# A hybrid attention, recurrence and mixture-of-experts layer on one core: fillers and ones-matmuls in the attention loop, another order at the hand-over, row gathers one turn later

## The reference

```
proj = x @ w_in                      # q, k, v of 8 attention heads; q, f, i, g of 8 recurrence heads
a = moba_attention(q, k, v, t5_bias) # causal block-sparse softmax attention, blocks of 256 keys
r = rms(hgrn2(q, f, i)) * norm_w * sigmoid(g)
x = layer_norm(alpha * x + concat(a, r) @ w_o)
g = top-1 of softmax over 4 groups;  e = top-2 of its 4 experts
y = sum over experts of weight * ((silu(x @ w_gate[e]) * (x @ w_up[e])) @ w_down[e])
x = layer_norm(alpha * x + y)
```

## Time and profile before

| | |
|---|---|
| median of 3 runs | 619.5 us (619.29 to 619.69) |
| the profiled execution, its own time | 619.69 us |
| its span, first to last instruction | 617.9 us |
| PE busy | 594.8 us (96%) |
| DVE busy | 479.2 us (78%) |
| ACT busy | 373.9 us (61%) |
| POOL busy | 127.1 us (21%) |
| mean granted TensorE clock | 0.987 |

### The profile page before, as it was taken

One profiled execution on the slowest core, in us unless ns is written; L12 is line 12 of the kernel. 1 busy time (PEld: TensorE's weight loads), 2 busy tenths in 40 slices (PEclk: granted clock), 3 DMA queues, 4 the chain that ended last, 5 costly groups with the idle time before them and its releaser, 6 DMA issues.

```text
span 617.9 us, 9761 instructions
## 1 busy us (share of the span) xinstructions
PE 594.8 (96%) x3691; PEld 479.2 (78%) x3691; DVE 479.2 (78%) x572; ACT 373.9 (61%) x401; POOL 127.1 (21%) x111
## 2 busy tenths in 40 slices
PE   8999999999999999999799999999999999999990
PEld 6878888888787678876688888888888888888870
DVE  3748598893577765556888989888888988888867
ACT  3659434432215983214378777877877787787735
POOL 0004222290000440000464722111110011111000
PEclk9999999999999999999899999999999999999996
DMA  8821133223206003975789999999999999999754
GB/s 326 294 97 66 62 126 124 77 73 77 70 2 204 3 2 132 416 282 205 247 321 420 418 372 368 390 389 390 408 406 390 389 389 387 392 409 404 249 171 136
DMA packets 42557, 155.77 MB, mean 252 GB/s; under 512 B 11939, under 2 KB 12147, under 8 KB 30236
## 3 DMA queue, kind: packets, MB, share of 16 engines
q1 hardware_dynamic: 37500, 138.40, 57.5%
q0 software_dynamic: 5024, 16.92, 10.6%
HBM read 139.96 MB, written 15.34 MB: 251 GB/s over the span
## 4 chain that ended last, share of the span: by engine, by line
PE 85%; DMA 6%; DVE 5%; issue 3%; ACT 1%; DVEq 0%; SPq 0%; POOLq 0%; ACTq 0%
PE psum L658 24%; PE psum L660 22%; PE psum L659 22%; DMA acc_dram<-misc,slots 3%; PE psum L771 2%; PE psum L1053 2%; PE psum L888 2%; PE psum L911 2%; PE psum L875 2%; DMA ring<-acc_dram 1%; PE psum L1070 1%; PE psum L667 1%; DVE w_lo L1775 1%; DMA cst<-in_c_main 1%; PE psum L813 1%
## 5 line engine op out<-in xcount | busy, mean ns | idle before, releaser
L1775 DVE TENSOR_TENSOR w_lo<-ring,w_hi 128x2048 fp32r<-128x2048 f32 x95 | 217.6, 2305 | 23.4 <-ACT w_hi L1345 21.1
L658 PE MATMUL psum<-w_hi,act_hi 128*128 128x512 f32 x544 | 219.6, 404 | 1.7 <-DVE act_lo L1934 1.0
L660 PE MATMUL psum<-w_hi,act_lo 128*128 128x512 f32 x544 | 213.0, 392 | 0.0
L659 PE MATMUL psum<-w_lo,act_hi 128*128 128x512 f32 x544 | 212.8, 391 | 0.0
L1345 ACT ACTIVATE w_hi<-ring 128x2048 fp32r<-128x2048 f32 x96 | 182.1, 1916 | 26.2 <-PE psum L660 25.1
L658 PEld LDWEIGHTS psum<-w_hi,act_hi 128*128 128x128 f32 x544 | 102.8, 189 | 28.3 <-DVE w_lo L1775 5.0
L660 PEld LDWEIGHTS psum<-w_hi,act_lo 128*128 128x128 f32 x544 | 102.4, 188 | 22.1
L659 PEld LDWEIGHTS psum<-w_lo,act_hi 128*128 128x128 f32 x544 | 102.7, 189 | 19.3
L612 POOL DMA_INDIRECT acc_dram<-misc,slots x15 | 23.9, 1596 | 192.7 <-ACT misc L1395 176.0
L1193 ACT ACTIVATE w_hi<-ring 128x2048 fp32r<-128x2048 f32 x17 | 32.6, 1917 | 49.1 <-PE psum L660 47.4
L1504 DVE TENSOR_TENSOR w_lo<-ring,w_hi 128x2048 fp32r<-128x2048 f32 x17 | 39.8, 2345 | 22.3 <-ACT w_hi L1193 22.1
(11 more groups left out here) (246 smaller groups left out, 686.5 us busy)
## 6 DMA issues: line engine op xcount, KB each, us to landing
ring<-in_w_gate SPq DMA_DIRECT2D x32, 1024.0 KB, 19.8
ring<-in_w_up SPq DMA_DIRECT2D x32, 1024.0 KB
ring<-in_w_down SPq DMA_DIRECT2D x32, 1024.0 KB, 20.5
ring<-in_w_in SPq DMA_DIRECT2D x13, 1024.0 KB, 5.4
ring<-in_w_o SPq DMA_DIRECT2D x4, 1024.0 KB, 6.7
acc_dram<-ring SPq DMA_DIRECT2D x5, 512.0 KB
ring<-in_x SPq DMA_DIRECT2D x2, 1024.0 KB, 6.5
ring<-strip_dram SPq DMA_DIRECT2D x8, 256.0 KB, 4.8
```

What stands on the lines that cost most here:

```text
L658: pe.matmul(dst, lh, rh, start=first, stop=False, skip_group_check=True)
L659: pe.matmul(dst, lh, rl, start=False, stop=False, skip_group_check=True)
L660: return pe.matmul(dst, ll, rh, start=False, stop=last, skip_group_check=True)
L1775: dve.tensor_tensor(w_lo[:, v0 % WBUF, :], ring[:, slot, :], w_hi[:, v0 % WBUF, :].bitcast(F32), ALU.subtract).then_inc(s_lo, 1)
```

## The change

It has three parts.

1. Attention loop. The scores of step 1 go to banks 4 and 5, with a wait for the logits of units 0 and 1, and `probs_t` loses its first two waits. 12 fillers stand ahead of the scores of step 1, and 10 each behind the scores of steps 1, 2 and 3. POOL writes diagonal 128x128 tiles (identity x reciprocal) into 8 buffers in place of the `wide` blocks, with a wait for the spread before, and `spread_scale` multiplies ones with them, in 8 matmuls in place of 4 transposes. `centred_router` moves from n = 8 to n = 4 on DVE.
2. Hand-over. SP's list of DMAs has another order and one wait more, for gather 1.
3. Expert loop. POOL issues gather(e + 2) in turn e in place of gather(e + 3).

```diff
@@ score banks, and the tiles
-        wide = misc[:, 3072:4096].rearrange("p (b i c) -> p b i c", b=2, i=T)
+        diag = misc[:, 3072:4096].rearrange("p (n c) -> p n c", c=P)
...
-            return (6 if step == 1 else 4 if step == 0 or step % 2 == 1 else 2) + n % 2
+            return (4 if step == 0 or step % 2 == 1 else 2) + n % 2
@@ SP
             expert_unit(step[5], 1, 0, 0)
-            sp.wait_ge(s_x1last, 1)
-            keep_tile(T - 1)
             sp.wait_ge(s_x1t, T + 1)
             sp.wait_ge(s_cent, T)
             expert_unit(step[3], 1, 0, 10)
+            sp.wait_ge(s_x1last, 1)
+            keep_tile(T - 1)
             sp.wait_ge(s_x1out, 16 * T)
-            sp.wait_ge(s_xg[0], 16)
-            expert_unit(step[4], 1, 0, 11)
+            for b in range(2):
+                sp.wait_ge(s_xg[b], 16)
             keep_sum(T - 1, T - 1)
             keep_sum(T - 1, T)
+            expert_unit(step[4], 1, 0, 11)
             sp.wait_ge(s_acc, 16 * (T + 1))
             expert_unit(step[0], 2, 1, 1)
@@ POOL
                 pool.wait_ge(s_prec, n // 2 + 1)
-                if n >= 4 * T:
-                    pool.wait_ge(s_scale, n // (2 * T) - 1)
-                pool.tensor_scalar(wide[:, n // (2 * T) % 2, i, 64 * (h % 2):64 * (h % 2) + 64], ones[:, 0:64], prec[:, col:col + 1], None, ALU.mult).then_inc(s_wide, 1)
+                if n >= DIAGS:
+                    pool.wait_ge(s_scale, 2 * (n // DIAGS))
+                pool.tensor_scalar(diag[:, n % DIAGS, :], ident, prec[:, col:col + 1], None, ALU.mult).then_inc(s_diag, 1)
...
             for e in range(NE - 1):
-                if EARLY < e + 3 < NE:
-                    gather(e + 3)
+                if EARLY < e + 2 < NE:
+                    gather(e + 2)
@@ PE
             def scores(n):
...
-                if n >= 6:
+                if n == 2:
+                    pe.wait_ge(s_logit, n)
+                elif n >= 6:
                     pe.wait_ge(s_logit, n - 2)
...
             def probs_t(n):
...
-                if n < 2:
-                    pe.wait_ge(s_logit, n + 3)
...
             def spread_scale(a):
...
                 for i in range(T):
-                    last = pe.transpose(psum[:, (a + 1) % 2, i * P:(i + 1) * P], wide[:, a % 2, i, :], ident)
-                last.then_inc(s_scale, 1)
+                    for par in range(2):
+                        last = pe.matmul(psum[64 * par:64 * par + 64, (a + 1) % 2, i * P:(i + 1) * P], ones[:, 0:64], diag[:, 2 * i + par, :],
+                                         start=True, stop=True, skip_group_check=True)
+                        if i == T - 1:
+                            last.then_inc(s_scale, 1)
...
             for n in range(0, NU + 4, 2):
+                if n == 2:
+                    keep_warm(12, 6)
                 if n < NU:
                     scores(n)
-                if n == 2:
+                if 2 <= n < 8:
                     pe.wait_ge(s_qklo, 2 * PAIRS)
-                    pe.wait_ge(s_router, 2)
-                    pe.matmul(psum[:, 1, 0:2 * KD * NL], ones, wg_b.rearrange("p r k n -> p (r k n)"), start=True, stop=True).then_inc(s_wsum, 1)
-                if n == 12:
+                    if n == 2:
+                        pe.wait_ge(s_router, 2)
+                        pe.matmul(psum[:, 1, 0:2 * KD * NL], ones, wg_b.rearrange("p r k n -> p (r k n)"), start=True, stop=True).then_inc(s_wsum, 1)
+                    keep_warm(10, 0)
+                if n == 10:
                     pe.wait_ge(s_router, 5)
@@ DVE
-                if n == 8:
+                if n == 4:
                     centred_router()
```

More of the change, by code:

```diff
@@ L48 @@
 EARLY = 4
+DIAGS = 8
 UNIT = 2048
@@ L320, in build @@
         s_tab, s_strip, s_stripsb, s_stripd, s_strips = sem("s_tab"), sem("s_strip"), sem("s_stripsb"), sem("s_stripd"), sem("s_strips")
-        s_score, s_logit, s_prob, s_wide, s_pt, s_ptsb, s_pv = sem("s_score"), sem("s_logit"), sem("s_prob"), sem("s_wide"), sem("s_pt"), sem("s_ptsb"), sem("s_pv")
+        s_score, s_logit, s_prob, s_diag, s_pt, s_ptsb, s_pv = sem("s_score"), sem("s_logit"), sem("s_prob"), sem("s_diag"), sem("s_pt"), sem("s_ptsb"), sem("s_pv")
         s_mixt, s_mixthi, s_mixtlo = sem("s_mixt"), sem("s_mixthi"), sem("s_mixtlo")
@@ L561, in _, with inverse_diagonal @@
                                pad_i[:, :, :]).then_inc(s_pads, 16)
-            def inverse_spread(n):
+            def inverse_diagonal(n):
                 h, i = unit(n)
@@ L567, in inverse_spread @@
                 pool.wait_ge(s_prec, n // 2 + 1)
-                if n >= 4 * T:
-                    pool.wait_ge(s_scale, n // (2 * T) - 1)
-                pool.tensor_scalar(wide[:, n // (2 * T) % 2, i, 64 * (h % 2):64 * (h % 2) + 64], ones[:, 0:64], prec[:, col:col + 1], None, ALU.mult).then_inc(s_wide, 1)
+                if n >= DIAGS:
+                    pool.wait_ge(s_scale, 2 * (n // DIAGS))
+                pool.tensor_scalar(diag[:, n % DIAGS, :], ident, prec[:, col:col + 1], None, ALU.mult).then_inc(s_diag, 1)
             for n in range(NU):
-                inverse_spread(n)
+                inverse_diagonal(n)
             def gather(e):
@@ L891, in spread_scale @@
             def spread_scale(a):
-                pe.wait_ge(s_wide, 2 * T * (a + 1))
+                pe.wait_ge(s_diag, 2 * T * (a + 1))
                 if a >= 1:
@@ L1710, in scale_kept @@
             def scale_kept(a):
-                dve.wait_ge(s_scale, a + 1)
+                dve.wait_ge(s_scale, 2 * (a + 1))
                 dve.tensor_copy(scale_row, bank((a + 1) % 2)).then_inc(s_mixa, 1)
```

## The result

The changed kernel takes 627.2 us at the median (625.5 to 628.8, 4 runs), the kernel before 619.4 in the same job: ratio 1.0122, with a 95% interval of 1.0095 to 1.0149. A later job of four runs gave 625.9 us and 1.0098 (1.0082 to 1.0113). With the profiled execution and one more, its ten executions took 625.5 to 628.8 us, 626.1 at the median. The forecast was 632.5, its range 625.0 to 635.5. So it is slower, by half to three fifths of the 13 us forecast. Two slow executions, one of the kernel before (843.5 us) and one of e2 (1186.5 us), enter no comparison.

The account below looks back on a forecast made before the run. PE, busy for 96% of the span, was taken to set the pace. Attention 6.0, gather 5's wait 5.5 and clock 1.5 made 13.0 us on 619.69, so 632.7, or 632.5 from the median; range 625.0 to 635.5.

Parts of the forecast that it names:

- gather(5) lands in time: Rival, expert loop: expert 5's rows land without making PE wait, leaving 619.5 + 6.0 = 625.5 us; 12%.
- First wait, 0.85: Attention, step 1: scores wait for logits of units 0 and 1, twelve fillers hidden under it; +0.85 us, bounds 0.4 and 1.3.
- Fillers, 3.3: Attention: 3 x 10 fillers between pieces of PE's chain, not hidden, 0.11 us each; +3.3 us, bounds 0 and 4.9.
- The rival of hidden fillers: Attention: unseen holes on PE hide the fillers, so 632.5 - 3.3 = 629.2 us; 6%.
- Spread, 1.9: Attention: eight matmuls at 1.02 us replace four transposes at 0.59, 0.44 in the last spread; +1.9 us, all on PE.
- attention's 6.0: Attention in all: 0.85 + 3.3 + 1.9 = +6.0 us on PE, shifting everything behind it.
- Clock in attention: Attention: granted clock already 1.00, so fillers and ones-matmuls have no lost clock to buy back.
- Hand-over, 0 (bound + 1): Hand-over: SP's new order delays the last x1 tile, covered by some 1 us; zero, without cover up to +1.
- Gather 5, 5.5, and its clock, 1.5: Expert loop: PE waits once for expert 5's rows, +5.5 us (4.3 to 5.9), then low clock, +1.5 (0 to 2).
- The margin in every turn: Rival, expert loop: the 2 us margin fails, gathers 6 to 15 cost 1 us each; 642.5 us, 5%.
- Clock, 1.5, elsewhere: Hand-over low clock, six matmuls costing 1.2 us, taken as model for +1.5 us behind expert 5's wait.

Follow-up runs that it names:

- e2: Kernel before with SP's new DMA order at the hand-over alone: 619.8 us, 1.0003.
- e7: Kernel before with only the 12 + 3 x 10 fillers added, old banks, waits and spread: 622.8 us, 1.0061.
- e8: Kernel before with the new spread alone (diagonal tiles, 8 matmuls of ones in place of 4 transposes): 620.0 us, 1.0012.
- e4: Kernel before with sum copies ahead of the slot-11 unit and the wait for gather 1, last tile still ahead of the slot-10 unit: 619.3 us, 0.9996.
- e5: Changed kernel with its gathers back in their old turn, gather(e + 3): 624.8 us, 1.0108.
- e9: Changed kernel measured again as it is, against the kernel before: 625.9 us, 1.0098.
- e3: Kernel before with the gathers one turn later alone, gather(e + 2): 625.6 us, 1.0103.
- e10: Kernel before with gathers from the sixth expert's on one turn later, gather 5 left in its old place: 620.0 us, 1.0010.
- e6: Changed kernel with SP's old DMA order, attention part and later gathers kept: 624.9 us, 1.0099.
- e12: Changed kernel with the last attention tile again ahead of the slot-10 weight unit, rest of SP's new order kept: 627.2 us, 1.0127.
- e1: Kernel before with the attention part of the change alone, SP's order and gathers as before: 624.9 us, 1.0091.
- e11: Kernel before with more fillers at the hand-over: 38 instead of 24 ahead of gather 0's wait, 8 more behind: 619.9 us, 1.0008.

## Right and wrong, step by step

The direction was right, and the measured time lies in the range, but by luck: the range had been drawn down to 625.0 to take in a rival at 12%, and 7 of the 13 us hung on a wait that is not there. The prediction said that it is wrong if that wait is missing, and by that it is wrong.

- **First wait, 0.85.** Right in size, wrong in cause. The scores of step 1 start at 200.98 (forecast 200.95), and L938 at 201.54 in place of 200.53, 1.0 later. But the twelve fillers were to be over at 200.75, hidden under the wait for logits; they last until the scores start, no wait is recorded, and in e7, which has no such wait, the delay is the same.
- **Fillers, 3.3.** Right: by starts the three groups cost 1.1 us each. With the first twelve PE is 4.2 us late at the scores of unit 8 (208.03 against 203.84) and 4.0 at the first spread. e7 is 3.5 us slower in time. The rival of hidden fillers is out.
- **Spread, 1.9.** Right in kind, mis-sized. The eight matmuls take the 1.02 us read from the earlier trace rows, but 0.15 of each comes back in the values behind them. By the chain it is 3 x 0.28 + 0.43 = 1.3 (the last spread grows from 0.44 to 1.02 and its values shrink from 1.02 to 0.87), and e8's trace has the same 1.3 in attention; e8's time is 0.7 longer (0 to 1.5). In all, attention's 6.0 was 5.3 on PE and 5.5 in time. That the values are quicker because they now follow matmuls of their own kind and not transposes is argued, not shown.
- **Clock in attention.** As the row had it: 1.00 before and after, with nothing bought back.
- **Hand-over, 0 (bound + 1).** Right at the median, by e2 and e4. In the profiled execution the cover of 1 us failed: the tile took 6.9 us behind the unit, and gather 0 went 1.5 late. In e2, e5 and e9, with the same order, it took 5.5, 5.8 and 6.1 us and held nothing, so it is a matter of the execution.
- **Gather 5, 5.5, and its clock, 1.5.** This step failed. The sum shifted POOL's issue times with nothing: it set 378.81 + 12.0 = 390.8 against PE's 385.25 of before, as if the 6.0 us of attention, which the same sum had put ahead of it, moved POOL's chain just as much. That did not happen. PE moved by 8.9 and gather 5's place by 0.8. The largest part of the difference is the 4.0 us of POOL's first copy and gather, short in every kernel with fillers; that it is the delay which takes them out from behind DVE's subtraction fits the traces but is argued, since no run moves the copy alone. In e3, without the delay, gather 5 left 2.0 us later than the sum had it and took 10.3 us, so it landed at 391.1 (the sum: 390.8). PE had come 1.2 us earlier than before, for its first turn took 7.86 us, and waited 7.08 us where 5.5 were forecast; the clock cost 1.3 for 1.5, and the time rose by 6.2, near the forecast 7.0. The rival "gather(5) lands in time", 625.5 at 12%, is what happened, though hardly through the door that it named: the scatter was faster by 0.8 of the 5.5 us needed, the rest is a POOL that was held up less and a later PE.
- **The margin in every turn.** Out: no wait for rows later in the loop, and e10 adds no measurable time.
- **Clock, 1.5, elsewhere.** A low stretch at the hand-over comes with and without the change, and its place differs between executions of one kernel; the first turn differs by up to 2.3 us with it (10.05 against 7.74). The forecast took it as given.

**Left open.** Attention gives 5.5 of the 6.4 to 7.8 us. A further 1.0 to 1.4 us shows up between experts 2 and 3 in all four profiled executions that have both the attention part and the later gathers (changed, e6, e9, e12), and in none of the five others of the table:

```profile
355.07 0.50 PE L660 MATMUL psum<-w_hi,act_hi 128*128 128x512 f32 x1 [0.94 <-DVE w_lo L1784]
```

```profile
351.10 3.91 DVE L1784 TENSOR_TENSOR w_lo<-ring,w_hi 128x2048 fp32r<-128x2048 f32 x1 [0.48 <-ACT w_hi L1354]
```

DVE's subtraction takes 3.91 us in place of 2.29 while POOL scales beside it (351.73, 2.87 above), and PE waits for it. The kernel before has such a subtraction too, but there PE does not wait:

```profile
348.34 3.79 DVE L1775 TENSOR_TENSOR w_lo<-ring,w_hi 128x2048 fp32r<-128x2048 f32 x1 [0.43 <-ACT w_hi L1345]
```

So the stretch alone does not make PE wait; which unit's subtraction it falls on may decide, which is not shown. In e1, e5 and e7 the scaling starts 0.81 to 1.04 us behind the subtraction and is itself the one stretched, to 3.98 to 4.21 us, and PE does not wait. For the subtraction at 351.10 the rule of the Trainium skill, SBUF — State Buffer, Who interferes with whom, told above, is not borne out: DVE had started first by 0.63 us and was the one held. Why the later gathers should shift that meeting, when POOL does the same up to it, no run tells, and since e6 has this wait and e5 has not, at the same 624.8, it may not be worth its size. That e6 and e5 lie 1.0 to 2.4 us under the changed kernel's two medians, with ranges that overlap, is not settled either: nothing measured here shows what SP's order or the later gathers are worth beside the attention part.

## What to carry to other kernels

When a sum has a delay early on and a race between two engines later, shift both sides of the race by it before taking the difference, and ask for each whether it is paced by the delayed engine or by something of its own, such as landings or another engine's work beside it; here one side moved 8.9 us and the other 0.8. A part measured alone tells what it does alone: later gathers cost 6.2 us on the old kernel and nothing that can be measured beside the attention part (e1 and e6, both 624.9). Fillers on an engine that is on the path and already at full clock are paid in full (e7: 4.2 us late on PE, grant 1.00).

## What was not expected of the hardware

- A POOL copy of 128 numbers took 0.19 us or 2.16, and the issue of a gather 1.02 or 3.02, and in thirteen of fourteen traces the two went together: long when DVE had just begun a subtraction of two 128x2048 tiles, short otherwise. When POOL's scaling meets that subtraction, it is DVE that is stretched with starts 0.33 to 0.75 us apart, and POOL with 0.81 to 1.04.
- The 512 KB write of a tile, issued by SP 1.6 us behind a 1 MB load, landed after 5.5 to 6.9 us in four traces; with the tile ahead it took 2.9. The prediction had allowed up to three times that.
- Filling PE's idle time at the hand-over did not remove its low-clock stretch: in e11 it lay on the fillers, and the time was the same.
